# State-space decays: the triangular mask held stationary, the scaled triangle streamed in 512 columns as a high and a low part

## The reference, cut to what matters

```python
a = -jnp.exp(a_log)
a_cum = jnp.cumsum(dtc * a, axis=2)                    # along the 128 positions of a chunk
seg = a_cum[:, :, :, None] - a_cum[:, :, None, :]      # [t, s]
decay = jnp.exp(jnp.where(causal, seg, -jnp.inf))
cb = jnp.einsum('bctgn,bcsgn->bctsg', cc, bc)
y_diag = jnp.einsum('bctsgh,bcsghp->bctghp', cb[..., None] * decay, xdt)
```

## Time and profile before

| | |
|---|---|
| median of 3 runs | 2354.15 us (2353.82 to 2355.65) |
| the profiled execution, its own time | 2353.8 us |
| span of its trace | 2352.0 us |
| PE busy | 2308.6 us, 98% of the span |
| DVE, ACT, POOL busy | 1453.5, 1305.4, 330.6 us |
| chain that ended last | PE 82%, DVE 9%, ACT 6%, POOL 2% |
| decays of the first of the two layers | PE from 1473.4 to 1504 us |
| decays of the second | PE from 1955.4 to 1986 us |

### The profile page before, as it was taken

How to read it: one execution, slowest core, us unless ns; L and a number is a source line. 1 busy time by engine, 2 the same in 40 slices (tenths; PEclk the granted TensorE clock), 3 DMA queues, 4 the chain that set the end, 5 groups by cost and what they waited for, 6 DMA issues and landing times.

```text
span 2352.0 us, 36560 instructions
## 1 busy us (share of the span) xinstructions
PE 2308.6 (98%) x15272; PEld 2067.4 (88%) x15272; DVE 1453.5 (62%) x2217; ACT 1305.4 (56%) x1958; POOL 330.6 (14%) x307
## 2 busy tenths in 40 slices
PE   7999999999999999999999999999999999999999
PEld 5799978888899888998789989899899898998998
DVE  6655555546645546546764567575677686765875
ACT  5554465555544556445564467565665675655654
POOL 0100032212100313001010002343000013530000
PEclk9999999999999999999999999999999999999999
DMA  6255443333455534555345544444455453444553
GB/s 266 90 212 183 179 178 138 141 134 126 179 190 187 197 141 157 196 182 203 113 173 186 194 178 148 144 162 162 179 187 189 175 184 126 162 164 160 201 193 126
DMA packets 58180, 398.92 MB, mean 170 GB/s; under 512 B 6816, under 2 KB 7072, under 8 KB 11680
## 3 DMA queue, kind: packets, MB, share of 16 engines
q1 hardware_dynamic: 56864, 393.75, 46.7%
q10 hardware_dynamic: 1152, 2.83, 0.3%
HBM read 395.51 MB, written 1.05 MB: 169 GB/s over the span
## 4 chain that ended last, share of the span: by engine, by line
PE 82%; DVE 9%; ACT 6%; POOL 2%; issue 1%; DMA 0%; SPq 0%; ACTq 0%; DVEq 0%; POOLq 0%
PE b L1280 12%; PE b L1282 12%; PE b L1281 12%; PE b L1178 12%; PE b L1179 12%; PE b L1180 12%; PE b L1183 5%; DVE wlo L1931 4%; PE b L1187 4%; ACT whi L1581 2%; ACT b L1577 1%; DVE xb L2229 1%; PE b L1246 1%; PE b L1247 1%; ACT S L1578 1%
## 5 line engine op out<-in xcount | busy, mean ns | idle before, releaser
L1931 DVE TENSOR_TENSOR wlo<-raw,whi 128x2048 fp32r<-128x2048 f32 x362 | 845.1, 2339 | 446.4 <-ACT whi L1581 446.1
L1581 ACT ACTIVATE whi<-raw 128x2048 fp32r<-128x2048 f32 x362 | 690.5, 1913 | 426.2 <-PE b L1282 221.9
L1280 PE MATMUL b<-xh,whi 128*128 128x256 f32 x2560 | 723.9, 283 | 1.0 <-DVE wlo L1931 0.7
L1282 PE MATMUL b<-xh,wlo 128*128 128x256 f32 x2560 | 712.4, 278 | 0.0
L1281 PE MATMUL b<-xl,whi 128*128 128x256 f32 x2560 | 711.6, 278 | 0.0
L1280 PEld LDWEIGHTS b<-xh,whi 128*128 128x128 f32 x2560 | 480.3, 188 | 5.6 <-DVE wlo L1931 3.3
L1281 PEld LDWEIGHTS b<-xl,whi 128*128 128x128 f32 x2560 | 481.4, 188 | 1.9
L1282 PEld LDWEIGHTS b<-xh,wlo 128*128 128x128 f32 x2560 | 481.1, 188 | 0.0
L1178 PE MATMUL b<-whi,xh 128*128 128x512 f32 x640 | 262.9, 411 | 1.5 <-DVE wlo L1931 1.5
L1178 PE MATMUL b<-whi,oh 128*128 128x512 f32 x656 | 259.0, 395 | 0.6 <-DVE ol L2220 0.6
L1179 PE MATMUL b<-wlo,oh 128*128 128x512 f32 x656 | 256.1, 390 | 0.0
(11 more groups left out here) (238 smaller groups left out, 2904.2 us busy)
## 6 DMA issues: line engine op xcount, KB each, us to landing
raw<-in_w SPq DMA_DIRECT2D x362, 1024.0 KB, 4.8
gt<-in_rows SPq DMA_DIRECT2D x8, 512.0 KB, 4.0
bt<-in_rows SPq DMA_DIRECT2D x8, 512.0 KB, 4.9
abq<-in_rows ACTq DMA_DIRECT2D x2, 768.0 KB, 6.3
x<-in_x SPq DMA_DIRECT2D x1, 1024.0 KB, 6.6
bc<-in_rows SPq DMA_DIRECT2D x4, 256.0 KB, 5.0
out<-x SPq DMA_DIRECT2D x4, 256.0 KB, 2.0
msk<-in_masks SPq DMA_DIRECT2D x1, 768.0 KB, 21.3
```

What stands on the lines that cost most here:

```text
L1280: pe.matmul(out, wh[:, k, cs], ah[:, kk, :], start=kk == 0 and s == 0, stop=False, skip_group_check=True)
L1282: last = pe.matmul(out, wl[:, k, cs], ah[:, kk, :], start=False, stop=final and k == 3, skip_group_check=True)
L1581: return ac.activation(out, i, ACT.Copy)
L1931: ve.tensor_tensor(B.wlo[r][:, :], B.raw[r][:, :], B.whi[s][:, :], ALU.subtract).then_inc(sem["loV"], 1)
```

## The change

PE's product is written the other way round. The mask `SL` becomes the stationary operand, as an fp32r copy `SLr` that is made once. What moves is `U` times `dA` of four heads, 512 columns in one instruction. It is split like the weights: `PT` (float32, now made by one DVE `tensor_tensor` with both operands broadcast), `dah` (its rounded copy in fp32r, made by ACT, one buffer) and `dal` (the rest, made by DVE, two buffers). PE multiplies `SLr` by `dah` and by `dal` into the same bank: two fp32r matmuls of 512 columns in place of four float32 matmuls of 128. The values 0 and 1 of the mask are exact in fp32r.

The steps are then `build`, `build_hi` (ACT; waits for `built` and for the matmuls of the group before to have finished, because `dah` is one buffer), `build_lo` (DVE; waits for `dahi`), and `decay` (PE; waits for `dalo`). `build_hi` of group n+1 is written right behind `decay` of group n; `build_lo` of n+1 and `build` of n+2 two yields later, behind `diag` of n-1.

```diff
             build(0)
+            high(0)
             yield
-            for n in range(8 + 2):
-                if n < 7:
-                    build(n + 1)
-                    yield
+            low(0)
+            build(1)
+            yield
+            for n in range(9):
                 if n < 8:
                     self.aux(("decay", l, n))
                     self.counts("decays", (l, n))
                     self.step("decay", l, n)
+                    high(n + 1)
                     yield
-                if 1 <= n < 9:
+                if n >= 1:
                     self.aux(("diag", l, n - 1))
                     self.step("diag", l, n - 1)
                     yield
+                low(n + 1)
+                build(n + 2)
+                yield
...
     def decay(l, n):
         b, m = use["decay", l, n]
-        p.wait_ge("built", mark["built", (l, n)])
+        p.wait_ge("dalo", mark["dalo", (l, n)])
+        p.wait_ge("later", 1)
         p.wait_ge(f"empty{b}", m)
-        for i in range(4):
-            last = mm(B.bank[b][:, 128 * i:128 * i + 128], B.PT[n % 2][:, 128 * i:128 * i + 128], B.U, i == 0, True)
-        last.then_inc(sem[f"full{b}"], 1)
+        pe.matmul(B.bank[b][:, :], B.SLr[:, :], B.dah[:, :], start=True, stop=False, skip_group_check=True)
+        pe.matmul(B.bank[b][:, :], B.SLr[:, :], B.dal[n % 2][:, :], start=False, stop=True,
+                  skip_group_check=True).then_inc(sem[f"full{b}"], 1)
...
+    def build_hi(l, n):
+        a.wait_ge("built", mark["built", (l, n)])
+        if n or l:
+            b, m = use["decay", *((l, n - 1) if n else (l - 1, 7))]
+            a.wait_ge(f"full{b}", m + 1)
+        copy(B.dah[:, :], B.PT[n % 2][:, :]).then_inc(sem["dahi"], 1)
+
...
-        for i in range(4):
-            last = ve.tensor_scalar(B.PT[n % 2][:, 128 * i:128 * i + 128], B.SL, B.dA[:, c, h0 + i:h0 + i + 1], None,
-                                    ALU.mult)
-        last.then_inc(sem["built"], 1)
+        if n == l == 0:
+            ve.tensor_copy(B.SLr[:, :], B.SL).then_inc(sem["later"], 1)
+        ve.tensor_tensor(B.PT[n % 2][:, :].rearrange("p (i n) -> p i n", i=4),
+                         B.U.unsqueeze(1).broadcast_to([128, 4, 128]),
+                         B.dA[:, c, h0:h0 + 4].unsqueeze(2).broadcast_to([128, 4, 128]),
+                         ALU.mult).then_inc(sem["built"], 1)
+
+    def build_lo(l, n):
+        v.wait_ge("dahi", mark["dahi", (l, n)])
+        ve.tensor_tensor(B.dal[n % 2][:, :], B.PT[n % 2][:, :], B.dah[:, :], ALU.subtract).then_inc(sem["dalo"], 1)
```

More of the change, by code:

```diff
@@ L918, in build, with high, low @@
             def build(n):
-                self.counts("built", (l, n))
-                self.step("build", l, n)
+                if n < 8:
+                    self.counts("built", (l, n))
+                    self.step("build", l, n)
+            def high(n):
+                if n < 8:
+                    self.counts("dahi", (l, n))
+                    self.step("build_hi", l, n)
+            def low(n):
+                if n < 8:
+                    self.counts("dalo", (l, n))
+                    self.step("build_lo", l, n)
             build(0)
+            high(0)
             yield
-            for n in range(8 + 2):
-                if n < 7:
-                    build(n + 1)
-                    yield
+            low(0)
+            build(1)
+            yield
+            for n in range(9):
                 if n < 8:
@@ L1911, in scalar_program @@
             "gelu_v": gelu_v, "gm_squares": gm_squares, "setup": setup, "tap_b": tap_b, "silu_b": silu_b,
-            "dt": dt, "softplus": softplus, "xs": xs, "ends": ends, "state": state, "decay": decay, "gelu_u": gelu_u,
+            "dt": dt, "softplus": softplus, "xs": xs, "ends": ends, "state": state, "build_hi": build_hi, "decay": decay, "gelu_u": gelu_u,
             "ya_hi": ya_hi, "z": z, "head_roots": head_roots, "rms_y": rms_y, "sigmoid": sigmoid,
@@ L2478, in vector_program @@
             "gm_norm": gm_norm, "setup": setup, "taps_b": taps_b, "softplus": softplus, "cb": cb, "off": off,
-            "build": build, "diag": diag, "mixed": mixed, "ya_lo": ya_lo, "head_roots": head_roots,
+            "build": build, "build_lo": build_lo, "diag": diag, "mixed": mixed, "ya_lo": ya_lo, "head_roots": head_roots,
             "head_scale": head_scale, "norm_y": norm_y, "join": join, "joined": joined, "yparts": yparts, "branch": branch,
@@ L2751, in __init__ @@
         big = sb("S", [128, 1600])
-        self.PT = several(2, "PT", [128, 512])
+        with ExitStack() as scaled:
+            self.PT = [sb(f"PT{i}", [128, 512], F32, scaled) for i in range(2)]
+        self.dal = several(2, "dal", [128, 512], F32R)
         self.m = several(4, "m", [128, 16])
@@ L2787, in __init__ @@
         self.qtmp = sb("qtmp", [128, 128])
+        self.SLr, self.dah = sb("SLr", [128, 128], F32R), sb("dah", [128, 512], F32R)
         self.ident, self.U, self.SL = self.con("ident"), self.con("U"), self.con("SL")
@@ L2841 @@
         "hhi", "hlo", "cva", "cvv", "gate", "xb", "vnorm", "wdh", "wdl", "lamv", "wst", "dtv", "dav", "xsg", "ea",
-        "xde", "offg", "built", "decays", "yam", "yahi", "yalo", "squares", "headn", "gz", "yn", "yog", "yhi",
+        "xde", "offg", "built", "dahi", "dalo", "later", "decays", "yam", "yahi", "yalo", "squares", "headn", "gz", "yn", "yog", "yhi",
         "mgg", "mgv", "mhi", "mlo"]
```

## The result

The changed kernel takes 2373.39 us (median of 4 runs, 2373.03 to 2373.65), the kernel before 2354.32 (2353.82 to 2355.65): 19.1 us longer, ratio 1.0081 with a 95% interval of 1.0068 to 1.0093. The forecast was 2365.7 with a range up to 2369.7. The sign and the places were right, the size was not: 11.5 us longer was forecast.

The account below looks back on a forecast made before the run. PE, busy 98% of the span, was taken as the bound. Waits of 9.3 us less 3.5 us saved per layer made 11.5 us over two layers with the mask's copy, so 2365.7 us, range 2359.5 to 2369.7.

Parts of the forecast that it names:

- What PE saves: Each decay on PE takes 0.46 us in place of 0.90, saving 0.44 us, times 16 groups = 7.0 us.
- Decay 0: First decay of a layer starts at 1474.78, not 1473.40, behind POOL and the DVE, ACT, DVE chain: 1.38 us lost.
- decay 1: Second decay waits 4.1 us, since ACT stands in its first rounding copy and all behind it is late.
- the rival in which the ports do not bind: DVE's new instructions run beside POOL's; decays 1, 5 and 7 come earlier, 4.9 us in all: 2360.8; chance 0.13.
- Decay 5: Waits 2.9 us, because DVE has a wlo ahead of its subtraction and POOL holds the ports.
- decay 7: Wanted at 1508.4, but POOL holds the ports until 1508.5 and DVE is done at 1509.2: 0.85 us wait.
- Decays 2 to 4 and 6: Subtractions done just in time for decays 2 to 4, 0.1 us allowed together; decay 6 in time.
- The sum: Per layer 9.3 us lost less 3.5 saved, 5.8 longer; 11.5 us over two layers with the mask copy.
- the clock falls in the long wait: Rival: PE's clock halves in the wait before decay 1, up to 1.7 us per layer more: 2369; chance 0.18.
- the chain is hidden: Rival: ACT is not held up and subtraction 5 precedes its wlo; only decay 0 is late: 2350.1; chance 0.06.

Follow-up runs that it names:

- experiment 4: Changed kernel with the subtraction of group n+1 and build of n+2 written ahead of diag n-1; 2365.84 us.
- experiment 2: Changed kernel with 18 unused filling matmuls on PE ahead of the wait of decay 1 only; 2368.98 us.
- experiment 3: Changed kernel with group 0's build, rounding copy and subtraction and group 1's build moved right behind the step xde; 2360.4 us.
- experiment 8: Against experiment 6: groups 0 and 1 built beside the two steps off, rounding copy two yields later, subtraction ahead of diag n-1; 2358.49 us.
- experiment 6: Changed kernel with two rounding buffers and each group prepared two decays ahead; 2354.67 us.
- experiment 10: Kernel before with the new product, but the small vector dA split once per layer and multiplied by U on DVE; 2349.42 us.
- experiment 1: Changed kernel with unused filling matmuls on PE, 18 ahead of the wait of decay 1 and 12 ahead of decay 5; 2366.22 us.
- 11: Kernel of experiment 10 with group 0 built earlier, two yields behind the step xde; 2349.28 us.

## Why the prediction was wrong in size

**What PE saves** was right: 7.0 us said, 7.6 measured by the product alone (4.5 to 10.1 by the interval), a decay 0.46 us long in the trace.

**Decay 0 and decay 1** were right to 0.03 us in their starts. At decay 0 some of that is luck. The forecast time leaves out the mask's copy, which only the sum adds, at 0.2 us; it cost 0.13 (waits of 2.01 us in the first layer and 1.88 in the second), and the rest of the chain was as much quicker. The cause of the long wait (ACT stands in its first rounding copy with everything else behind it) is shown by moving that copy: the wait fell from 3.76 to 0.81 us. DVE's wait for POOL at the ports is in the trace (1.34 us for a subtraction of 0.68), so the rival in which the ports do not bind is out.

**Decay 5** was right in its cause, shown by moving the subtraction, and near in size. The trace counts idle time from the end of the last matmul, the forecast counts from the next possible start, 0.16 us earlier; counted its way the waits are 3.9 us at decay 1 (4.1 forecast; PE also came 0.15 us later than assumed), 2.7 at decay 5 (2.9) and 0.5 at **decay 7** (0.85). Decays 2 to 4 and 6 waited for nothing, where 0.1 us was allowed.

**The sum** failed at one step, the rival "the clock falls in the long wait". It stands in the prediction as another way that things might go, at a chance of 0.18, at up to 1.7 us per layer and at decay 1 alone, and the upper end of the range, 2369.7, follows from that. It is a term of the sum. The clock falls at decay 1 and at decay 5 too, which costs 2.4 + 1.6 = 4.0 us per layer by the rows of the changed kernel, and 3.9 by the layer in which the fills kept the clock. I took its size from eight matmuls at the start, 1.6 us, and did not ask what it costs where dense work follows: there PE loses as long as the low clock lasts. With it the sum closes: decay 7 was forecast for 1509.3 and started at 1512.84 in the old clock (1513.83 - 0.99), 3.5 us later. That is the clock's 4.0 and 0.2 for the slower starts after the waits, less 0.7 for waits behind decay 1 that were shorter than forecast. The 5.7 us forecast per layer and these 3.5 are 9.2, against 9.3 measured.

What the prediction puts against this rival is wrong as a reading of its own trace. It says that the trace has one such case only, at the start, and none in the middle of dense work. There is a second case in the middle of the kernel before, after an idle time of 1.93 us and with dense work on both sides (the last row is of the windows view):

```profile
1383.64 1.70 PE L1187 MATMUL b<-cst,xn 128*128 128x128 f32 x8 [1.93 <-DVE xn L2050]
1386.37 0.77 PE L1246 MATMUL b<-whi,xh 128*128 128x512 f32 x1 [1.03 <-issue]
...
1390.77 0.41 PE L1246 MATMUL b<-whi,xh 128*128 128x512 f32 x1
...
1386.00:1389.00 3.00, 2.63 (x6) 2.15 (x7) 1.96 (x4) 2.05 (x7) 0.00 (x0) 0.50 0.01 3
```

The ten matmuls from 1386.37 to 1390.77 take 4.40 us, where 0.23 each would be 2.3, and the eight of 1383.64 take 1.70 us where eight of the same form at full clock take 1.03 (1392.19). By an estimate from these rows, less 0.1 for the start after the idle time, that fall cost 2.7 us. With it the rival of one fall per layer would have been at 2365.7 + 5.4 = 2371.1 and one of two falls at 2376.5; the measured 2373.4 lies between them.

The Trainium skill's rule beside that rival (TensorE: Matmul & The Clock Gate, "Part 1: The HAM clock gate") was the better guide: an idle array falls back to half its clock. The trace agrees: 0.50 granted at 1483 to 1488.

The rival "the chain is hidden" came out as a kernel of its own, not as this change: with the chain taken out by the split of the vector, 2349.4 us, near the 2350.1 of that rival, since there too only decay 0 is late.

## What to carry to other kernels

Where PE is busy for 98% of the time, a long wait in the middle can cost its length and then the clock, and the second part belongs in the sum. Here a wait of 3.76 us cost 2.4 to 2.5 us more in each of four places, and one of about 2.5 us cost 1.6 more in five of six. Look for earlier falls in the whole trace, not only around the change. An engine that stands in a wait holds up all that is queued behind it, and its arrival there, not the length of its new instruction, is what to compute. Before a large operand is split into high and low parts through two more engines, look whether it is a product with a mask of 0 and 1: then the small factor can be split once, and the chain is gone.

## What the runs showed that I had not expected

The clock did not follow the length of the wait alone. In the decays of the profiles read here it fell at all four waits of 3.76 us (the changed kernel and experiment 4), at five of the six of 2.5 to 2.6 us (the changed kernel and experiments 2 and 3), at one of the two of 2.10 us in experiment 8, at two of the four of 1.7 to 1.8 us that the fills left, at none of the four of 1.5 to 1.7 us in experiments 6 and 10, and at none of the eight of 1.9 to 2.1 us before decay 0 (the changed kernel and experiments 1, 2 and 4). What decides it was not tested.

Matmuls that nobody uses can pay: 18 + 12 of them per layer, 3.6 us of PE's time in each, took 7.2 us off the changed kernel. They do not beat the kernel before (2366.2 us against 2353.8).

Where DVE and POOL meet, each added product on DVE can last much longer than alone: 0.68 us became 1.78 beside POOL's additions in experiment 8 and 2.38 in experiment 3. DVE's extra work came back as PE's wait for POOL in experiments 6 (1.65 us) and 11 (0.55 us), whose decays themselves waited for nothing.
